# Weight-unit splits behind the exponent and the scaled probabilities in the attention stage, one unit a step sooner, one output unit ahead of the last tile splits

## The reference

```python
def attn_fourier_layer(x, ctx, c, c_ctx, ..., w_in, sink, w_f, w_out, need_ctx_out):
    shift, scale, gate = adaln(c, w_mod, b_mod)          # silu(c) @ w_mod + b_mod
    h = rmsnorm(x, norm_g) * (1.0 + scale[:, None]) + shift[:, None]
    q, k, v, f, z = jnp.split(h @ w_in, SPLIT0, axis=-1)
    ...                                                   # rotary on q, k; kc, vc of the context
    y = jnp.concatenate([windowed_attention(q, k, v, kc, vc, sink), fourier_mix(f, w_f)], axis=-1)
    x = x + gate[:, None] * ((y * jax.nn.silu(z)) @ w_out)
def pool_layer(...):
    x = x + gate[:, None] * pool_branch(h, w_in, w_grp, layer_scale, w_out)
def reference(...):
    ...
    return rmsnorm(x, final_norm)
```

## Time and profile before

| | |
|---|---|
| median of 3 runs | 1442.05 us (1441.32 to 1442.59) |
| the profiled execution | 1441.64 us, its span 1440.0 us |
| TensorE busy | 1409.8 us, 98% of the span |
| TensorE weight loads busy | 1183.1 us, 82% |
| DVE busy | 904.3 us, 63% |
| ACT busy | 501.6 us, 35% |
| POOL busy | 77.1 us, 5% |
| granted clock of TensorE, mean | 0.998 |
| attention stage | about 386 to 678 us, some 72 us a head |

### The profile page before, as it was taken

The page is one execution under the profiler, slowest core; times in us unless marked ns, Lnnn a source line. Parts: engine busy times, 40 slices in busy tenths (PEclk is TensorE's granted clock), DMA queues, the critical chain, the costliest instruction groups (busy, mean ns, idle before and its releaser), DMA issues.

```text
span 1440.0 us, 20122 instructions
## 1 busy us (share of the span) xinstructions
PE 1409.8 (98%) x7714; PEld 1183.1 (82%) x7714; DVE 904.3 (63%) x1422; ACT 501.6 (35%) x730; POOL 77.1 (5%) x148
## 2 busy tenths in 40 slices
PE   5999999999999999999999999999999999999997
PEld 3788888888888888888888888888888888888897
DVE  6645656456767687776556676664555666674456
ACT  5223322244555344444222342112351323332233
POOL 0001111011100000000010001000000000010000
PEclk9999999999999999999999999999999999999999
DMA  9996667557611333324666656333323232366345
GB/s 384 408 385 223 197 214 255 165 177 217 206 58 54 105 109 115 117 75 158 204 193 191 199 177 205 117 91 100 99 92 102 88 101 90 98 197 191 104 145 174
DMA packets 65099, 236.87 MB, mean 164 GB/s; under 512 B 7232, under 2 KB 8128, under 8 KB 63744
## 3 DMA queue, kind: packets, MB, share of 16 engines
q1 hardware_dynamic: 43344, 157.83, 33.2%
q0 software_dynamic: 19712, 72.03, 16.0%
q10 hardware_dynamic: 1968, 5.95, 1.2%
HBM read 231.59 MB, written 4.19 MB: 164 GB/s over the span
## 4 chain that ended last, share of the span: by engine, by line
PE 93%; DVE 5%; issue 1%; ACT 1%; DMA 0%; DVEq 0%; ACTq 0%
PE ps L1385 91%; PE ps L1613 2%; DVE w_lo L798 1%; DVE kvmem L944 1%; DMA vec<-in_vectors 0%; DVE stat L1065 0%; DVE pooled L1346 0%; DVE kvmem L860 0%; DVE tmp L917 0%; DVE pt_lo L1104 0%; DVE modchunk L805 0%; DVE main L921 0%; DVE tmp L1076 0%; ACT scratch L533 0%; DVE h_lo L870 0%
## 5 line engine op out<-in xcount | busy, mean ns | idle before, releaser
L1385 PE MATMUL ps<-h_hi,w_hi 128*128 128x512 f32 (+1 forms) x1664 | 643.2, 387 | 1.0 <-DVE w_lo L798 0.5
L1385 PE MATMUL ps<-h_hi,w_lo 128*128 128x512 f32 (+1 forms) x1664 | 634.6, 381 | 0.0
L1385 PE MATMUL ps<-h_lo,w_hi 128*128 128x512 f32 (+1 forms) x1664 | 634.2, 381 | 0.0
L798 DVE TENSOR_TENSOR w_lo<-raw,w_hi 128x1024 fp32r<-128x1024 f32 x216 | 264.3, 1224 | 358.4 <-ACT w_hi L437 358.0
L437 ACT CAST w_hi<-raw 128x1024 fp32r<-128x1024 f32 x216 | 226.5, 1049 | 646.1 <-PE ps L1385 646.0
L1385 PEld LDWEIGHTS ps<-h_hi,w_hi 128*128 128x128 f32 x1664 | 312.9, 188 | 63.7 <-issue 5.4
L1385 PEld LDWEIGHTS ps<-h_hi,w_lo 128*128 128x128 f32 x1664 | 312.8, 188 | 61.2
L1385 PEld LDWEIGHTS ps<-h_lo,w_hi 128*128 128x128 f32 x1664 | 313.2, 188 | 56.8 <-issue 0.2
L805 DVE CUSTOM_DVE_ANT_0 modchunk<-modchunk,cond_row 128x1024 f32<-128x1024 f32 x128 | 154.8, 1219 | 21.1 <-DMA modchunk<-in_modb 21.1
L392 POOL DMA_DIRECT2D modchunk<-in_modb x128 | 67.6, 528 | 1140.2 <-DVE modacc L805 1115.8
L641 ACT CAST pt_hi<-ps 128x512 fp32r<-128x512 f32 (+1 forms) x48 | 30.7, 639 | 124.1 <-PE ps L1613 124.1
(11 more groups left out here) (206 smaller groups left out, 1343.5 us busy)
## 6 DMA issues: line engine op xcount, KB each, us to landing
raw<-in_weights SPq DMA_DIRECT2D x216, 512.0 KB, 3.6
modchunk<-in_modb POOLq DMA_DIRECT2D x128, 512.0 KB, 4.6
raw<-in_mod SPq DMA_DIRECT2D x32, 512.0 KB, 8.6
modchunk<-in_mod SPq DMA_DIRECT2D x16, 512.0 KB, 7.2
cond_row<-in_mod SPq DMA_DIRECT2D x16, 512.0 KB, 9.0
main<-in_xT SPq DMA_DIRECT2D x4, 1024.0 KB, 8.9
main<-in_xT ACTq DMA_DIRECT2D x4, 1024.0 KB, 4.9
out<-pooled SPq DMA_DIRECT2D x14, 256.0 KB, 2.1
```

Of the source, the lines that this page charges most:

```text
L798: nc.vector.tensor_tensor(w_lo[:, j % 2], src, w_hi[:, j % 2].bitcast(F32), ALU.subtract).then_inc(lo_ready, 1)
L1385: return nc.tensor.matmul(out, lhsT, rhs, start=start, stop=stop, skip_group_check=True)
```

## The change

Three edits, on ACT and DVE alike:
1. In `attention` the unit of a step (w_hi on ACT, w_lo on DVE) stands behind the exponent, respectively behind the scaled probabilities, instead of in front of q, the turned tiles and these. On ACT in head 0 it stands in front of `swap`.
2. `UNIT_SLOTS` has 10 in place of 11: the eighth unit of a group (index 5 of the slots counting from 0 is `hi(n, 7)`) is split in step 10. The sixth pair of mixed tiles in head 3 goes with the slot. `JOB_SLOTS` has 11 in place of 10, so that it names 11 twice: jobs 4 and 5 both run in step 11. The loop over the slots is written so that a slot may stand twice.
3. Third unit of the first output group (`hi(G_O, 2)`, `lo(G_O, 2)`) in front of the splits of the last four mixed tiles; `group` gets `begun`, with which it leaves that unit out.

```diff
@@ -127,9 +127,9 @@
-UNIT_SLOTS = (2, 4, 6, 7, 9, 11, 13)
+UNIT_SLOTS = (2, 4, 6, 7, 9, 10, 13)
 QUERY_SLOTS = (2, 5, 8)
-JOB_SLOTS = (1, 3, 5, 8, 10, 11, 12)
+JOB_SLOTS = (1, 3, 5, 8, 11, 11, 12)
 BANK_STEPS = (3, 2, 2, 2, 3, 2, 2, 3, 2, 2, 3, 2, 2, 2)
 assert sum(BANK_STEPS) == GROUP * HALVES
@@ -461,10 +461,11 @@
                     ins = nc.scalar.activation(dst, x, ACT.Identity, bias=bias)
                 ins.then_inc(split_hi, 1)
-            def group(n, b, evac=None, ctx_banks=None, side=None, grp=0):
+            def group(n, b, evac=None, ctx_banks=None, side=None, grp=0, begun=False):
                 for s in range(HALVES - 1):
-                    hi(n, s + 2, grp=grp)
+                    if s or not begun:
+                        hi(n, s + 2, grp=grp)
                     if side:
                         side(s)
                 if evac:
@@ -628,9 +629,6 @@
                     if k == 1:
                         piece(v_hi[:, 0:BLOCKS], values[:, :, bass.ds(i * P, P)])
                         piece(v_hi[:, BLOCKS:], values_c[:, :, bass.ds(i * P, P)])
-                    if k in UNIT_SLOTS:
-                        s = UNIT_SLOTS.index(k)
-                        hi(i + G_Z, s + 2)
                     if k in QUERY_SLOTS:
                         n = QUERY_SLOTS.index(k) + 1
                         if n >= 2:
@@ -641,6 +639,9 @@
                         nc.scalar.copy(*turned_tiles(k - 1, pt_hi)).then_inc(pt_hi_ready, 1)
                     if k < STEPS and (k or first):
                         exponent(i, k)
+                    if k in UNIT_SLOTS:
+                        s = UNIT_SLOTS.index(k)
+                        hi(i + G_Z, s + 2)
                     if first and k % 3 == 1 and k < 3 * GROUP:
                         m = k // 3
                         swap(3 * GROUP + m, main[:, 3 * GROUP + m], scratch, 3 * GROUP + m)
@@ -668,6 +669,7 @@
             attention(KV_HEADS - 1, last=True)
+            hi(G_O, 2)
             for t in range(EARLY, KT):
                 split(H_MIX0 + t, main[:, t], h_hi[:, t])
@@ -686,7 +688,7 @@
                 def reload_beside(s):
                     if s == 1:
                         reload_x(3)
-                group(G_O + i, B_O + i, side=(reload_beside, None, None, scale_beside)[i])
+                group(G_O + i, B_O + i, side=(reload_beside, None, None, scale_beside)[i], begun=i == 0)
                 residual_squares(B_O + i, SUM_0 + i * GROUP, i * GROUP)
             for m in range(GROUP):
                 scaled_hi(EARLY + m)
@@ -835,10 +837,11 @@
                             reduced(cg)
                 return at
-            def group(n, jobs=None, finish=None, side=None, last=False):
+            def group(n, jobs=None, finish=None, side=None, last=False, begun=False):
                 for s in range(HALVES - 1 if not last else HALVES - 2):
-                    lo(n, s + 2)
+                    if s or not begun:
+                        lo(n, s + 2)
                     if jobs:
                         jobs(s)
                     if side:
@@ -1089,10 +1092,6 @@
                     if k == 1:
                         piece(i * PIECES + 4, v_lo[:, 0:BLOCKS], values[:, :, bass.ds(i * P, P)], v_hi[:, 0:BLOCKS])
                         piece(i * PIECES + 5, v_lo[:, BLOCKS:], values_c[:, :, bass.ds(i * P, P)], v_hi[:, BLOCKS:])
-                    if k in UNIT_SLOTS:
-                        s = UNIT_SLOTS.index(k)
-                        if s < HALVES - 2 or last:
-                            lo(i + G_Z, s + 2)
                     if k in QUERY_SLOTS:
                         n = QUERY_SLOTS.index(k) + 1
                         piece(i * PIECES + (5 + n), q_lo[:, n % 2],
@@ -1105,8 +1104,13 @@
                                                 ALU.subtract).then_inc(pt_ready, 1)
                     if k < STEPS and (k or first):
                         probabilities(i, k)
-                    if k in JOB_SLOTS and not (first or last):
-                        job(i + (M_Z - 1), JOB_SLOTS.index(k))
+                    if k in UNIT_SLOTS:
+                        s = UNIT_SLOTS.index(k)
+                        if s < HALVES - 2 or last:
+                            lo(i + G_Z, s + 2)
+                    for j, slot in enumerate(JOB_SLOTS):
+                        if slot == k and not (first or last):
+                            job(i + (M_Z - 1), j)
                     if last and k in UNIT_SLOTS and UNIT_SLOTS.index(k) < EARLY // 2:
                         for t in (2 * UNIT_SLOTS.index(k), 2 * UNIT_SLOTS.index(k) + 1):
                             split(H_MIX0 + t, main[:, t], h_hi[:, t], h_lo[:, t])
@@ -1144,6 +1148,7 @@
             attention(KV_HEADS - 1, last=True)
+            lo(G_O, 2)
             for t in range(EARLY, KT):
                 split(H_MIX0 + t, main[:, t], h_hi[:, t], h_lo[:, t])
@@ -1172,7 +1177,7 @@
                                                    op0=ALU.add, op1=ALU.mult).then_inc(gain_ready, 1)
                     nc.vector.tensor_scalar(vec[:, V_LS:V_SINK], vec[:, V_LS:V_SINK], 0.5, None, ALU.mult)
                 group(G_O + i, set_of_jobs(M_O + i), lambda: residual(B_O + i, i * GROUP, 0),
-                      side=(clear_beside, None, None, scale_beside)[i])
+                      side=(clear_beside, None, None, scale_beside)[i], begun=i == 0)
                 add_squares(SQ_0 + i * GROUP, SUM_0 + i * GROUP)
             for m in range(GROUP):
                 scaled_lo(EARLY + m)
```

## The result

The changed kernel takes 1448.59 us (median of 6 runs, 1448.19 to 1449.05); the kernel before beside it 1441.9. The ratio is 1.0044, 95% interval 1.0033 to 1.0055: slower by about 6.4 us (the two medians differ by 6.7). The forecast was 1446.9, slower.

What follows compares the result with a forecast made beforehand. TensorE, busy 1409.8 of 1440.0 us, bounds the kernel, with DVE setting the end of heads 1 and 2. Terms -0.56 + 6.36 - 0.45 + 0.20 - 0.71 = +4.84 us on the median 1442.05 gave 1446.9, range 1444.0 to 1451.0.

Steps and rivals of the forecast that it cites:

- the wait of job 6: End of heads 1 and 2: job 6's load is issued late, so DVE and TensorE lose 3.18 us each time.
- head 0: Turn of step 11 in head 0: probabilities ready sooner without w_lo in front, -0.56 of a 0.80 us stall.
- the jobs: Jobs 4 and 5 both in step 11 of heads 1 and 2: job 6 delayed, +6.36 us in all.
- head 3: Turn of step 11 in head 3: splits moved to step 10 make the maximum begin late, +0.20 us.
- the output unit: Third unit of the first output group: its 0.69 us stall waiting for w_lo goes, -0.71 us.
- the turn's stall: Turn of step 11 in heads 1 and 2: a stall of 0.26 us goes, counted within the 3.18 us.
- rival (B): TensorE's clock falls in the pauses before heads 2 and 3: 2.7 us more per head, 1452.3 us; chance 10%.
- the prediction's own last line: Prediction wrong if job 6 starts right behind pt_lo, or the clock is below 1 in the two pauses.
- q_lo in head 2: Scores of step 3 in head 2: q_lo goes ahead of w_lo, the 0.43 us stall goes, -0.45 us.
- The fourth unit's margin: Fourth unit, split in step 4 of each head: w_lo ready 0.4 us before TensorE begins it, cost 0.
- rival (C): Moved units come late in four heads, say 0.3 us each: +1.2 on the sum, 1448.1 us; chance 8%.

Runs made afterwards that it cites:

- e1: The changed kernel with jobs 4, 5 and 6 again in steps 10, 11 and 12; 1442.42 us against 1441.97 for the kernel before.
- e2: The kernel before with only jobs 4 and 5 both put in step 11; 1451.34 us, ratio 1.0065.
- e8: The changed kernel with job 6 in step 13 instead of 12; 1441.66 us beside 1442.24 for the kernel before.
- e5: The changed kernel with two unused fp32 products on TensorE at the end of heads 1, 2 and 3; 1448.34 us against 1448.59.
- e7: e6 with step 1's v_lo pieces behind the probabilities and head 3's last mixed-tile splits kept in step 11; 1438.05 us, ratio 0.9969 to the kernel before.
- e4: The kernel before with only the unit moved behind exponent and probabilities, slots unchanged; 1442.42 us beside 1442.24.
- e3: The kernel before with only the first output group's third unit moved in front of the last four splits; 1441.13 us beside 1442.24.
- e9: The kernel before with only the job slots changed to 3, 3, 6, 6, 9, 9, 11; 1440.69 us beside 1442.20.
- e6: The changed kernel with job slots 3, 3, 6, 6, 9, 9, 11; 1439.81 us, ratio 0.9982 to the kernel before.

## Why the prediction held, point by point
The time came out in the range because the largest term, the wait of job 6, was right in mechanism and size. The clock's 2.0 us were put at nothing in the sum; that the time is only 1.7 above it is in part luck, since the other terms together came out 0.25 us lower than forecast (+0.21 for head 0, -0.29 for the jobs, +0.03 for head 3, -0.20 for the output unit). The prediction also says that the output stages hold no stall within reach, and then counts one there.
- **Job 6 waits for its load.** The step that decided the sign was right in its parts: lag from job to issue 0.65 us (0.65), landing 3.9 us (4.1 taken), no idle time on DVE behind it to take it up. The first units of heads 2 and 3 came 3.08 and 3.22 - 0.23 = 2.99 us later against 3.18 each (both with the turn's stall taken off). Shown by e1, e2 and e8. The page "DMA: Bandwidth & Descriptors" of the Trainium skill has a fit (section "Anatomy of one DMA — SWDGE (gpsimd) path") that makes an estimate of 3.2 us for such a load. The rows of this case are longer: 3.9 here, up to 5.4 for others in the attention stage, and by part 6 of the profile's page a median of 4.6 over all 128.
- **The clock.** This is the term that was left out of the sum and stood as rival (B), at 10%. By the prediction's own last line it is the point where it was wrong: the clock did fall at the start of both heads. The size, 0.4 + 1.6 = 2.0 us, is more than the 1.7 that the sum lacked. I had priced it at 2.7 a head and called it unlikely, since neither pause by itself is long. That it comes of the pause is shown by e5. In head 2 it cost only 0.4, though eight matmuls ran 0.2 us longer each (1.6): in e5 and in the kernel before TensorE waits for DVE in the first steps of the head (0.57 us at the turn of step 1 in e5), in the changed kernel it does not, so the slow matmuls ran in that time. In head 3 twelve ran slow (2.5 us) and less waiting stood ready to hide them. It isn't the two pauses taken together that count, as one would think from head 2 alone. Of the four falls, two here and two in e2, three lie in the scores, behind a first pause of 2.2 to 2.6 us and ahead of the second (the one in head 3 of e2 by 0.1 us only). The page "TensorE: Matmul & The Clock Gate" of the Trainium skill (table "Why this matters for your kernels") asks for no idle gaps above about 3 us between bursts of matmuls. These rows do not agree with it: a single pause of 2.2 us was enough.
- **Head 0.** 0.35 us came of the 0.56. ACT was the limit, as said, but the exponent ended 0.2 us later than counted: at 450.24 it begins behind the end of pt_hi (449.63 + 0.59), where before it had begun 0.1 us under it, and w_hi in front of swap shifted pt_hi by some 0.07. The term was the right one and too large.
- **Head 3.** +0.23 against +0.20: the maximum starts at 675.50, behind two h_lo (674.30, 1.29 us), and the turn keeps a stall of 0.27 + 0.16 us. e7 took it away.
- **q_lo in head 2** came in time; the stall of 0.43 is gone in the changed kernel and in e4. It doesn't show in the table only because the clock's loss lies in the same stretch: with the -0.45 forecast, the -0.06 measured leaves 0.39 for the clock, and e5 gave 0.45.
- **The fourth unit's margin.** w_lo was ready 0.49 us before its unit in heads 1 to 3 where 0.4 was counted; rival (C) cost nothing.
- **Output unit.** -0.71 forecast; -0.91 in the changed kernel's last stretch and, from the same two points, -0.47 in e3. The stall itself is gone in both. Over all runs that stretch takes 770.2 to 770.3 us without the edit (the kernel before, e2, e9) and 769.3 to 770.0 with it (the changed kernel, e1, e3, e6, e7, e8), so the edit gave some 0.5 us, less than the 0.71; where the rest went is open.

What stays open: why the clock stayed low for 6.8 us in head 3 (from about 610.8 to 617.6 us) and for 3.4 in head 2. It is not the head that decides, since in e2 it is 6.8 us in both; the short one is the only one of the four that began in the second pause. The runs don't separate the causes. That the chunk's load could be issued sooner with a third buffer was not tried.

## What to carry to other kernels
Before an instruction that uses a double-buffered load is moved later, look up who refills its buffer and how far behind the next user of that buffer stands: two users brought together in one step save nothing, and here one issue and landing, 0.65 + 3.9 us, became the distance that was missing. The price is paid where the waiting engine is full up to a point that the bounding engine (here TensorE) waits for; a wait that follows a stretch without idle time passes through in full, and one step further on, as job 6 in step 13, the same work is nearly free. And a pause of TensorE should be counted with what the clock does behind it.

## What the runs showed of the hardware
- The clock fell to 0.50 behind a pause of 2.3 us with 1.1 us of scores after it, in the second pause, and stood there from about 535.7 to 539.1 us (head 2). Behind a pause of 2.2 us it fell in the scores and stood there from 610.8 to 617.6 (head 3). In e2 it fell in the scores both times (in head 3 at their very end), behind 2.6 us, for 6.8 us. With the first pause cut to 0.3 and 0.5 us (e5) it did not fall, though the second, of 1.1 to 1.2 us, was left.
- In the changed kernel two loads of 512 KB issued by GpSimd 1.15 us apart took 3.9 us for the first, as most single ones in heads 1 and 2 do, and 4.9 and 4.6 for the second. In e6 four of the six first ones of a pair took 4.5 to 4.8, and a load with its neighbour 3.5 us away took up to 4.8 (e1). Over all 128 loads of the kernel the median is 4.6, so a margin worked out from 3.9 is smaller than it looks.
